# RWKV scan: order of TensorE's products among the inverses' steps, place of the bonus, buffers and time of y's factors

## The chip, the cores and the metric

One of the eight cores of a Trainium2 chip runs the whole program in one launch. The metric is the device time of that core in microseconds (us). Lines are those of the kernel before.

## The reference

The reference is a two-layer network on 256 tokens of width 1024, followed by a second block (window attention, stick-breaking attention, a PEER layer). The change touches only its RWKV-7 mixer in layer 0, with 16 heads of 64:

```
r, k, v = einsum(h + dx * mu[:3], w_rkv)
...
y = wkv7_scan(heads(r), heads(decay), heads(k), heads(v), -kk, kk * a_h)
mean = mean(y, -1);  var = mean((y - mean)**2, -1)
y = ((y - mean) * rsqrt(var + eps)) * ln_g + ln_b
bonus = sum(heads(r) * heads(k) * r_k, -1)
y = y + bonus * heads(v)
return (y * g) @ w_o
```

The scan goes over the tokens with a state of 64x64 per head. The kernel computes it in two blocks of 128 tokens (tb 0 and 1) by matrices: the token-by-token products MAK, MRK, MRB and MT (masked), the inverse of a unit lower triangular matrix made of MT (TIT is its transpose), then w, u = TIT w, the state S0 between the blocks, and y.

## The kernel before, in words

All weights stream as 128x1024 tiles (512 KB each, line 164, from SyncE's queue) through four raw slots. ScalarE makes the rounded high part of each (line 182), VectorE the low part (line 194; from `in_q_a` on every third on GpSimd, line 206), and TensorE multiplies with both (lines 252 to 254, 295 to 299). w_v's tiles are used whole. No tile scheduler is involved: each engine has its order written out by hand, and engines meet at semaphores.

TensorE's order in the scan stands in `tensor_scan`. The inverses come in steps of a generator, `tensor_inverses`: X5 of both blocks (line 952, 32x32 products), then TIT5 and TI5 (lines 964 and 966), X6 of block 0 in two halves (line 975), X6 of block 1 together with TIT6 of block 0 (lines 975 and 978), and TIT6 of block 1 (line 978). ScalarE takes block 0's results out (line 1560), VectorE block 1's (line 1290), and each step needs the one before taken out. "Products" MAK, MRK and MRB (line 933) are 16 small matmuls for each block and kind, taken out with a mask by VectorE in four pieces (line 1285). w, u and y are added by `add` (line 1053): eight matmuls of 128x128 weights on 64 columns for a half. Every matmul of plain f32 stands as two instructions in the trace, so w of a half has 16. `tensor_bonus` (line 870) has 16 matmuls, 32 instructions.

PSUM has eight banks, handed out in turn by `bank` (line 230): who takes a bank waits until its last content, eight banks ago, has been taken out. So any insertion or move in TensorE's order changes who waits for whom.

GpSimd makes the factors of y in `pool_factors`: four operations on 128x1024 for each block (lines 1640, 1643, 1645, 1647), once the gains `ln` have been loaded (line 754, 1 MB, issued after the bonus is done and after the first four tiles of w_o).

VectorE's order in the scan stands in `vector_scan`: after the inverses, the masks of MRK and MRB of block 0, the low parts of w_o's first three tiles (line 194, after ScalarE has made the high parts behind u of block 0), the state S0 (lines 1309 and 1314), centring (lines 1342 to 1349), the twelve masks of block 1, y's norm.

Of the kernel before, what the change touches and what calls it, by code (L numbers as in the profile page):

```python
# [16 lines left out]
P = 128  # L17
# [653 lines left out]
def rwkv_rooms(k):  # L671
# [13 lines left out]
        b_tok=u(1)[:, 0:D], k_tok=u(1)[:, D:2 * D], S0=u(1)[:, 0:D], wbuf=late[:, 0, 0:D], ubuf=late[:, 0, D:2 * D],  # L685
        ln=late[:, 1, :], y=u(5)[:, 0:D], y2=u(5)[:, D:2 * D], u=u,
        MT=matrices(arena[:, 9:11, :], P), TIT=matrices(arena[:, 12:14, :], P), TI=matrices(arena[:, 14:15, :], HD),
        MAK=[matrices(arena[:, n:n + 1, :], P) for n in (5, 11)], MRB=[matrices(arena[:, 9 + tb:10 + tb, :], P) for tb in range(TB)],
        MRK=[matrices(arena[:, 0:1, :], P)] * TB, X5=matrices(r["spare"][:, 0:1, 0:D], SMALL),
        X6=matrices(r["spare"][:, 1:2, :], HD), diagonal=u(5)[:, 0:D].rearrange("p (q t) -> p q t", t=SMALL), blocks=u(11)[:, 0:D].rearrange("p (i j) -> p i j", j=SMALL),  # L690
# [71 lines left out]
def tensor_rwkv(k):  # L762
# [175 lines left out]
def tensor_inverses(k):  # L938
# [7 lines left out]
    for tb in range(TB):  # L946
# [6 lines left out]
        ins.then_inc(*k.level_products.mark(("X5", tb, 0), ("X5", tb, 1)))  # L953
    yield
    tensor.wait_ge(*k.small_turned.at("TIT"))
    for tb in range(TB):
# [10 lines left out]
        ins.then_inc(*k.level_products.mark(("TIT5", tb, 0), ("TIT5", tb, 1), ("TI5", tb)))  # L967
    yield
    low, up = rows_of(0, 2), rows_of(2, 2)
# [10 lines left out]
    for half in range(2):  # L980
        ps = bank(k, ("X6", 0, half), out[0], ("X6", 0, half))
        for m in range(8):
            ins = first(ps, 8 * half + m, slice(m * HD, (m + 1) * HD))
        ins.then_inc(*k.level_products.mark(("X6", 0, half)))
        yield
    tensor.wait_ge(*out[1].at(("TI5", 1)))
# [53 lines left out]
def tensor_scan(k):  # L1040
# [52 lines left out]
    def state():  # L1093
# [8 lines left out]
        ins.then_inc(*k.state_done.mark("state"))  # L1102

    inverses = tensor_inverses(k)
    next(inverses)
    tensor_bonus(k)
    next(inverses)
    w(0, 0)
    next(inverses)
    w(0, 1)  # L1110
    next(inverses)
    next(inverses)
    tensor_scan_tokens(k)
    next(inverses)
    tensor_scan_products(k, 0, "MRK", "k_s", "r_s", k.masked)
    tensor_scan_products(k, 0, "MRB", "b_s", "r_s", k.masked)
    for half in range(2):
        u(0, half)
    state()
    tensor_scan_products(k, 1, "MAK", "k_s", "a_s", k.masked)  # L1120
    for half in range(2):
        y(0, half, y_known(0, half))
    tensor_scan_products(k, 1, "MRB", "b_s", "r_s", k.masked)
    tensor_scan_products(k, 1, "MRK", "k_s", "r_s", k.masked)
    for half in range(2):
# [4 lines left out]
    known.append(y_known(1, 1))  # L1130
    for half in range(2):
        y(1, half, known[half])
    for half in range(2):
        tensor_turn_y(k, 0, half)

# [143 lines left out]
def vector_scan(k, substitute):  # L1279
# [16 lines left out]
    vector.transpose(r["straight"], r["inverse"].rearrange("p i j -> p j i")).then_inc(*k.small_turned.mark("TI"))  # L1296
    vector.transpose(r["turned"], r["inverse"]).then_inc(*k.small_turned.mark("TIT"))
    steps = take_out_inverses(k, 1, copy)
    next(steps)
    vector.wait_ge(*k.bonus_done.at("bonus"))  # L1300
    vector.tensor_copy(r["bonus"], result(k, "bonus")[:, 0:TB * HEADS]).then_inc(*k.scaled.mark("bonus"))
    for _ in steps:
        pass
    masked("MRK", 0, r["upto"])
    masked("MRB", 0, r["upto"])
    split_low(k, FIRST["w_o"][0] + SLOTS)
    S0, ps = r["S0"], result(k, "state")
    vector.wait_ge(*k.state_done.at("state"))
# [9 lines left out]
    vector_centring(k)  # L1318
    vector.wait_ge(*k.small_copied.at("TIT"))
    vector.wait_ge(*k.small_turned.now())  # L1320
    masked("MAK", 1, r["strict"])
    masked("MRB", 1, r["upto"])

    vector.wait_ge(*k.per_head_done.at(("y", 0, 1)))
    masked("MRK", 1, r["upto"])
    for _ in zip(vector_head_norm(k, 0), vector_head_norm(k, 1)):
        pass
    for half in range(2):
        vector_head_var(k, 1, half)
    for half in range(2):  # L1330
        vector_y_low(k, 0, half)
    for _ in zip(vector_last_norm(k, 0), vector_last_norm(k, 1)):
# [29 lines left out]
def vector_head_norm(k, half):  # L1362
# [21 lines left out]
    vector.wait_ge(*done.now())  # L1384
    vector.tensor_tensor(yh, yh, r["y2"][:, cols], ALU.add).then_inc(*k.y_made.mark((0, half)))
    yield


def vector_last_norm(k, half):
# [12 lines left out]
    vector.wait_ge(*done.now())  # L1402
    vector.tensor_tensor(yh, yh, r["y2"][:, cols], ALU.add).then_inc(*k.y_made.mark((1, half)))
    yield
# [145 lines left out]
def scalar_scan(k):  # L1550
# [12 lines left out]
    next(steps)  # L1563
    next(steps)
    for half in range(2):
        per_head("w", 0, half, r["wbuf"])
        next(steps)
    next(steps)
    for name, dst in (("b", r["b_tok"]), ("k", r["k_tok"])):
        for i in range(2):  # L1570
            scalar.wait_ge(*k.tokens_turned.at(name + str(i)))
            scalar.activation(dst[:, half_of(i)], result(k, ("tok", name, i)), ACT.Copy).then_inc(
                *k.tokens_out.mark((name, i)))
    for half in range(2):
        per_head("u", 0, half, r["ubuf"])
# [7 lines left out]
    for half in range(2):  # L1583
        per_head("u", 1, half, r["ubuf"])
    for half in range(2):
        scalar_head_squares(k, 1, half)
    for tb in range(TB):
        for half in range(2):
            scalar_y_high(k, tb, half)


def pool_rwkv(k):
# [17 lines left out]
    for quarter in (2, 3, 0, 1):  # L1610
# [3 lines left out]
        pool.wait_ge(*k.small_copied.now())  # L1614
    pool_factors(k, 0)
    for half in range(2):
        pool_head_root(k, 0, half)
    pool_factors(k, 1)
    for half in range(2):
        pool_head_root(k, 1, half)  # L1620

# [7 lines left out]
def pool_factors(k, tb):  # L1629

    pool, r, done = k.pool, k.room["rwkv"], k.factors_made
    g_of, y2 = r["g_tok"][:, tb, :], r["y2"]
    pool.wait_ge(*k.loaded["ln"].at("ln"))
    pool.wait_ge(*k.scaled.at("bonus"))
    pool.wait_ge(*k.v_out.at(("w_v", tb, 1)))
    if tb:
        pool.wait_ge(*k.y_made.at((0, 1)))
    else:
        pool.wait_ge(*k.per_head_done.at(("w", 0, 1)))
    pool.tensor_tensor(by_head(y2), by_head(r["v_tok"][:, tb, :]), spread(r["bonus"][:, tb * HEADS:(tb + 1) * HEADS], HD),  # L1640
                       ALU.mult).then_inc(*done.mark())
# [1640 lines left out]
```

## Time and profile before

| | |
|---|---|
| median of 3 runs | 2251.96 us (2251.47 to 2253.64) |
| profiled execution, own time | 2245.33 us |
| its span in the trace | 2244.0 us |
| TensorE busy | 2129.6 us, 95% of the span |
| VectorE, ScalarE, GpSimd busy | 1558.4, 1108.9 and 348.3 us |
| mean granted clock of TensorE | 0.963 of 2.4 GHz |

Times of the trace count from the start of the span. The RWKV mixer's scan lies between 335.8 us, when w_v's last product has been issued, and 422.9 us, when w_o's first starts. The granted clock is 1.00 (2.4 GHz) or 0.50 (1.2 GHz) at any time. A busy TensorE says little by itself: matmuls overlap, so the distance between starts counts.

### The profile page before, as it was taken

The numbers are of one execution on the slowest core, as the hardware profiler recorded it, in microseconds if no ns is written. First come the engines' busy times: TensorE is split into PE (matmuls) and PEld (weight loads), VectorE is DVE, ScalarE is ACT, GpSimd is POOL, SyncE is SP. The second block draws the span as 40 slices with busy tenths as digits, with TensorE's granted clock in tenths as the row PEclk, the third lists the DMA queues.
The fourth block names the chain that finished last, engine by engine and source line by source line (L and its number), as shares of the span: only waits on it lengthen the run. The fifth ranks groups of instructions, "written<-read, shape, count | busy, mean of one in ns | idle before, by whom it ended". The sixth has DMA issues, their size and how long they took to land.

```text
span 2244.0 us, 33802 instructions
## 1 busy us (share of the span) xinstructions
PE 2129.6 (95%) x13292; PEld 1861.4 (83%) x13292; DVE 1558.4 (69%) x2589; ACT 1108.9 (49%) x1757; POOL 348.3 (16%) x165
## 2 busy tenths in 40 slices
PE   8997999999999999799999878999999999999999
PEld 6886788888878887578888656999999999888887
DVE  5667784676676666866675775688999995555554
ACT  5554632265555555555554774444444444444443
POOL 0000102200010001100004102223222222222222
PEclk9998997999999999689999889999999999999999
DMA  5665231156645565146655224444544445656664
GB/s 197 190 188 178 85 113 58 50 181 187 192 161 181 192 187 173 45 126 192 188 186 192 86 66 156 163 161 160 170 150 142 145 142 175 196 195 192 193 191 158
DMA packets 97630, 352.52 MB, mean 157 GB/s; under 512 B 10897, under 2 KB 12689, under 8 KB 97089
## 3 DMA queue, kind: packets, MB, share of 16 engines
q1 hardware_dynamic: 97472, 350.36, 48.9%
q8 instruction: 107, 1.75, 0.3%
q14 instruction: 51, 0.41, 0.1%
HBM read 349.26 MB, written 1.05 MB: 156 GB/s over the span
## 4 chain that ended last, share of the span: by engine, by line
PE 81%; DVE 13%; ACT 3%; issue 2%; POOL 1%; DMA 0%; SPq 0%; ACTq 0%; DVEq 0%
PE psum L252 17%; PE psum L253 16%; PE psum L254 16%; PE psum L296 14%; PE psum L295 6%; DVE tile_low L194 3%; PE psum L2586 2%; PE psum L1053 1%; PE psum L856 1%; ACT tile_high L182 1%; PE psum L299 1%; POOL small L1665 1%; DVE hT L488 1%; PE psum L338 1%; DVE peer_active L2781 1%
## 5 line engine op out<-in xcount | busy, mean ns | idle before, releaser
L194 DVE TENSOR_TENSOR tile_low<-raw_tiles,tile_high 128x1024 fp32r<-128x1024 f32 x535 | 662.5, 1241 | 368.4 <-ACT tile_high L182 361.8
L182 ACT ACTIVATE tile_high<-raw_tiles 128x1024 fp32r<-128x1024 f32 x642 | 677.7, 1056 | 447.2 <-PE psum L254 447.0
L296 PE MATMUL psum<-hT,tile_high 128*128 128x512 f32 x1408 | 494.7, 395 | 5.6 <-issue 5.0
L206 POOL TENSOR_TENSOR tile_low<-raw_tiles,tile_high 128x1024 fp32r<-128x1024 f32 x107 | 269.9, 2522 | 761.9 <-ACT tile_high L182 761.9
L252 PE MATMUL psum<-hT,tile_high 128*128 128x256 f32 x1280 | 372.9, 291 | 8.0 <-DVE tile_low L194 3.9
L253 PE MATMUL psum<-hT,tile_high 128*128 128x256 f32 x1280 | 365.5, 286 | 0.0
L254 PE MATMUL psum<-hT,tile_low 128*128 128x256 f32 x1280 | 365.2, 285 | 0.0
L252 PE MATMUL psum<-tile_high,hT 128*128 128x512 f32 (+1 forms) x848 | 336.7, 397 | 22.6 <-DVE mix_arena L2402 9.3
L295 PE MATMUL psum<-hT,tile_low 128*128 128x256 f32 x1232 | 344.2, 279 | 0.0
L253 PE MATMUL psum<-tile_low,hT 128*128 128x512 f32 (+1 forms) x848 | 333.0, 393 | 0.0
L254 PE MATMUL psum<-tile_high,hT 128*128 128x512 f32 (+1 forms) x848 | 333.0, 393 | 0.0
L296 PEld LDWEIGHTS psum<-hT,tile_high 128*128 128x128 f32 x1408 | 258.9, 188 | 55.2 <-issue 6.1
L252 PEld LDWEIGHTS psum<-hT,tile_high 128*128 128x128 f32 x1280 | 249.0, 195 | 9.6 <-issue 8.0
L253 PEld LDWEIGHTS psum<-hT,tile_high 128*128 128x128 f32 x1280 | 249.2, 195 | 0.0
L254 PEld LDWEIGHTS psum<-hT,tile_low 128*128 128x128 f32 x1280 | 248.8, 194 | 0.0
L295 PEld LDWEIGHTS psum<-hT,tile_low 128*128 128x128 f32 x1232 | 232.8, 189 | 8.9
L252 PEld LDWEIGHTS psum<-tile_high,hT 128*128 128x128 f32 x848 | 162.4, 192 | 62.6 <-issue 15.1
L254 PEld LDWEIGHTS psum<-tile_high,hT 128*128 128x128 f32 x848 | 162.0, 191 | 33.8
L253 PEld LDWEIGHTS psum<-tile_low,hT 128*128 128x128 f32 x848 | 162.5, 192 | 32.5
L252 PE MATMUL psum<-tile_high,ffn_hidden_high 128*128 128x512 f32 x352 | 139.3, 396 | 2.5 <-DVE ffn_hidden_low L657 2.5
L253 PE MATMUL psum<-tile_low,ffn_hidden_high 128*128 128x512 f32 x352 | 139.0, 395 | 0.0
L254 PE MATMUL psum<-tile_high,ffn_hidden_low 128*128 128x512 f32 x352 | 139.0, 395 | 0.0
(334 smaller groups left out, 2541.8 us busy)
## 6 DMA issues: line engine op xcount, KB each, us to landing
raw_tiles<-ffn_in_dram SPq DMA_DIRECT2D x176, 512.0 KB, 3.6
raw_tiles<-peer_u_dram SPq DMA_DIRECT2D x128, 512.0 KB, 3.3
raw_tiles<-peer_v_dram SPq DMA_DIRECT2D x128, 512.0 KB, 4.0
raw_tiles<-ffn_out_dram SPq DMA_DIRECT2D x88, 512.0 KB, 3.5
raw_tiles<-w_kv_dram SPq DMA_DIRECT2D x16, 512.0 KB, 3.4
raw_tiles<-in_gates_dram SPq DMA_DIRECT2D x16, 512.0 KB, 3.3
raw_tiles<-peer_q_dram SPq DMA_DIRECT2D x16, 512.0 KB, 3.4
raw_tiles<-w_k_dram SPq DMA_DIRECT2D x8, 512.0 KB, 4.1
```

The costliest lines, as they stand in the source:

```text
L182: scalar.activation(k.high[:, n % SLOTS, :], k.raw[:, n % RAW_SLOTS, :], ACT.Copy).then_inc(*k.tile_high_made.mark(n))
L194: vector.tensor_tensor(k.low[:, n % SLOTS, :], k.raw[:, n % RAW_SLOTS, :], k.high[:, n % SLOTS, :].bitcast(F32), ALU.subtract).then_inc(*k ...
L206: pool.tensor_tensor(k.low[:, n % SLOTS, :], k.raw[:, n % RAW_SLOTS, :], k.high[:, n % SLOTS, :].bitcast(F32), ALU.subtract).then_inc(*k.p ...
L252: k.tensor.matmul(out, still[0], moving[0], start=first, stop=False)
L253: k.tensor.matmul(out, still[0], moving[1], start=False, stop=False)
L254: return k.tensor.matmul(out, still[1], moving[0], start=False, stop=last)
L295: k.tensor.matmul(ps[:, 0:T], low[:, c, :], both[:, c, 0, :], start=False, stop=False, skip_group_check=True)
L296: ins = k.tensor.matmul(ps, high[:, c, :], both[:, c, :, :], start=(c == 0), stop=(c == KC - 1), skip_group_check=True)
L299: k.tensor.matmul(ps[:, 0:T], low[:, c, :], both[:, c, 0, :], start=False, stop=False, skip_group_check=True)
L338: ins = k.tensor.transpose(ps[:, c * P:(c + 1) * P], src[:, c * P:(c + 1) * P], k.ident)
L488: vector.scalar_tensor_tensor(out=k.hT[1][:, c, :], in0=result(k, ("x", s, c))[:, 0:T], scalar=gain_of(k, s, c), in1=k.hT[0][:, c, :].bitc ...
L2586: ins = tensor.matmul(ps[:, n, :], r["i_hot"](q)[:, :, n], r["j_gates"](q)[:, n // 2, w, :, n % 2], start=(w == 0), stop=(w == PARTS - 1))
```

## The change

- `tensor_bonus` moves from behind X5 to between w_v's two halves.
- `tensor_inverses` pauses after each block's X5 and after each block's TIT5, and no more between the two halves of X6 of block 0: seven steps. Between them stand w(0,0), w(0,1), MRK of block 0, the turned tokens, MAK of block 1, MRB of block 0.
- MRB of block 1 comes before the state, MRK of block 1 between the state and y of block 0.
- MRK has two buffers (units 0 and 14), y2 too (units 5 and 4).
- GpSimd makes both blocks' factors before the first root. Block 1's wait for MRB of block 1 (the last reader of unit 4), where before they waited for y of block 0 to be finished.
- VectorE's masks follow the new order: MRB of block 1 stands between w_o's low parts and the state, MRK of block 1 behind the centring.
- y of block 0 is turned before the last products of y of block 1; ScalarE's and VectorE's orders follow.

```diff
-        MRK=[matrices(arena[:, 0:1, :], P)] * TB,
+        MRK=[matrices(arena[:, n:n + 1, :], P) for n in (0, 14)],
...
     for g in range(2):
+        if g:
+            tensor_bonus(k)
         ps = [bank(k, ("w_v", tb, g), k.v_out, ("w_v", tb, g)) for tb in range(TB)]
...
     inverses = tensor_inverses(k)
-    next(inverses)
-    tensor_bonus(k)
     next(inverses)
     w(0, 0)
     next(inverses)
     w(0, 1)
     next(inverses)
+    tensor_scan_products(k, 0, "MRK", "k_s", "r_s", k.masked)
     next(inverses)
     tensor_scan_tokens(k)
     next(inverses)
-    tensor_scan_products(k, 0, "MRK", "k_s", "r_s", k.masked)
+    tensor_scan_products(k, 1, "MAK", "k_s", "a_s", k.masked)
+    next(inverses)
     tensor_scan_products(k, 0, "MRB", "b_s", "r_s", k.masked)
+    next(inverses)
     for half in range(2):
         u(0, half)
+    tensor_scan_products(k, 1, "MRB", "b_s", "r_s", k.masked)
     state()
-    tensor_scan_products(k, 1, "MAK", "k_s", "a_s", k.masked)
+    tensor_scan_products(k, 1, "MRK", "k_s", "r_s", k.masked)
     for half in range(2):
         y(0, half, y_known(0, half))
-    tensor_scan_products(k, 1, "MRB", "b_s", "r_s", k.masked)
-    tensor_scan_products(k, 1, "MRK", "k_s", "r_s", k.masked)
     for half in range(2):
         w(1, half)
...
     for half in range(2):
+        tensor_turn_y(k, 0, half)
+    for half in range(2):
         y(1, half, known[half])
-    for half in range(2):
-        tensor_turn_y(k, 0, half)
...
     masked("MRK", 0, r["upto"])
+    next(steps)
+    vector.wait_ge(*k.small_copied.at("TIT"))
+    vector.wait_ge(*k.small_turned.now())
+    masked("MAK", 1, r["strict"])
+    next(steps)
+    next(steps)
     masked("MRB", 0, r["upto"])
+    next(steps)
     split_low(k, FIRST["w_o"][0] + SLOTS)
+    masked("MRB", 1, r["upto"])
     S0, ps = r["S0"], result(k, "state")
...
     vector_centring(k)
-    masked("MAK", 1, r["strict"])
-    masked("MRB", 1, r["upto"])
-    vector.wait_ge(*k.per_head_done.at(("y", 0, 1)))
     masked("MRK", 1, r["upto"])
...
-    pool_factors(k, 0)
-    for half in range(2):
-        pool_head_root(k, 0, half)
-    pool_factors(k, 1)
-    for half in range(2):
-        pool_head_root(k, 1, half)
+    for tb in range(TB):
+        pool_factors(k, tb)
+    for tb in range(TB):
+        for half in range(2):
+            pool_head_root(k, tb, half)
...
-    if tb:
-        pool.wait_ge(*k.y_made.at((0, 1)))
-    else:
-        pool.wait_ge(*k.per_head_done.at(("w", 0, 1)))
+    pool.wait_ge(*(k.scan_products.at(("MRB", 1, 1)) if tb else k.per_head_done.at(("w", 0, 1))))
```

## Rows read from the trace of the kernel before

**Rows 1.** The page: busy time of the engines, and the chain that ended last.

```profile
PE 2129.6 (95%) x13292; PEld 1861.4 (83%) x13292; DVE 1558.4 (69%) x2589; ACT 1108.9 (49%) x1757; POOL 348.3 (16%) x165
PE 81%; DVE 13%; ACT 3%; issue 2%; POOL 1%; DMA 0%; SPq 0%; ACTq 0%; DVEq 0%
```

**Rows 2.** Busy time of the engines, granted clock (PEclk) and DMA by stretches.

```profile
340.00:346.00 6.00, 6.00 (x40) 5.96 (x42) 1.16 (x3) 0.00 (x0) 1.82 (x1) 0.53 0.00 0
352.50:364.00 11.50, 11.44 (x80) 11.02 (x81) 2.05 (x3) 1.79 (x3) 1.71 (x1) 0.50 0.01 2
364.00:367.50 3.50, 3.50 (x65) 3.38 (x62) 0.72 (x2) 1.21 (x3) 3.34 (x3) 0.50 0.02 5
396.40:418.00 21.60, 21.60 (x195) 21.59 (x194) 12.27 (x23) 4.02 (x7) 8.11 (x5) 1.00 0.00 1
423.00:429.00 6.00, 6.00 (x14) 4.75 (x15) 4.26 (x7) 0.00 (x0) 2.38 (x2) 0.50 0.00 0
```

**Rows 3.** Timeline of TensorE, inverses: start, us, what, count, idle before and releaser.

```profile
335.84 3.80 PE L952 MATMUL psum<-rwkv_spare,rwkv_arena 32*32 32x32 f32 x128
339.57 6.31 PE L870 MATMUL psum<-rwkv_masks,rwkv_late 128*128 128x16 f32 x32
...
352.56 0.26 PE L964 MATMUL psum<-rwkv_arena,rwkv_spare 32*32 32x32 f32 x1 [2.63 <-issue]
...
352.94 3.68 PE L1053 MATMUL psum<-rwkv_arena 128*128 128x64 f32 x16
356.54 1.97 PE L975 MATMUL psum<-rwkv_arena 64*64 64x64 f32 x16
...
369.38 2.08 PE L978 MATMUL psum<-rwkv_arena,rwkv_spare 64*64 64x64 f32 x32
```

**Rows 4.** DMA issues between 345 and 352 us: KB, us to landing.

```profile
rwkv_late<-ln_dram SPq DMA_DIRECT2D x1, 1024.0 KB, 5.0
```

**Rows 5.** Timeline of TensorE, from the products to w_o.

```profile
371.39 3.84 PE L933 MATMUL psum<-rwkv_arena 64*128 64x128 f32 x64
...
379.72 0.34 PE L1100 MATMUL psum<-rwkv_late,rwkv_arena 128*64 128x64 f32 x4 [0.78 <-ACT rwkv_late L1555]
...
381.76 2.06 PE L933 MATMUL psum<-rwkv_arena 64*128 64x128 f32 x32
...
393.23 3.25 PE L933 MATMUL psum<-rwkv_arena 64*128 64x128 f32 x48 [1.04 <-DVE rwkv_arena L1285]
396.41 10.93 PE L1053 MATMUL psum<-rwkv_arena 128*128 128x64 f32 x96
...
422.94 0.77 PE L252 MATMUL psum<-tile_high,hT 128*128 128x512 f32 x1 [3.99 <-DVE hT L1423]
```

**Rows 6.** Timeline of VectorE between 380 and 400 us.

```profile
380.69 3.50 DVE L194 TENSOR_TENSOR tile_low<-raw_tiles,tile_high 128x1024 fp32r<-128x1024 f32 x3 [3.22 <-ACT tile_high L182]
384.35 0.91 DVE L1309 MEMSET rwkv_arena<- 128x1024 f32 x1 [0.16 <-issue]
...
391.80 7.26 DVE L1285 TENSOR_TENSOR rwkv_arena<-psum,rwkv_masks 128x512 f32<-128x512 f32 x12
```

**Rows 7.** Timeline of GpSimd: two of the four operations of block 1's factors.

```profile
413.01 1.90 POOL L1640 TENSOR_TENSOR rwkv_arena<-rwkv_arena,small 128x1024 f32<-128x1024 f32 x1 [3.81 <-DVE rwkv_arena L1385]
414.99 2.35 POOL L1643 TENSOR_TENSOR rwkv_arena<-rwkv_arena,rwkv_late 128x1024 f32<-128x1024 f32 x1
```

**Rows 8.** GpSimd and VectorE side by side, at 1503 us and at 1541 us.

```profile
1503.39 2.38 POOL L206 TENSOR_TENSOR tile_low<-raw_tiles,tile_high 128x1024 fp32r<-128x1024 f32 x1 [4.53 <-ACT tile_high L182]
...
1503.81 3.05 DVE L194 TENSOR_TENSOR tile_low<-raw_tiles,tile_high 128x1024 fp32r<-128x1024 f32 x1
...
1541.43 1.22 DVE L194 TENSOR_TENSOR tile_low<-raw_tiles,tile_high 128x1024 fp32r<-128x1024 f32 x1
1542.56 3.42 DVE L2781 TENSOR_TENSOR peer_active<-peer_active 128x1024 f32<-128x1024 f32 x1
...
1541.63 3.28 POOL L206 TENSOR_TENSOR tile_low<-raw_tiles,tile_high 128x1024 fp32r<-128x1024 f32 x1 [4.73 <-ACT tile_high L182]
```

More of the change, by code:

```diff
@@ L685, in rwkv_rooms @@
         b_tok=u(1)[:, 0:D], k_tok=u(1)[:, D:2 * D], S0=u(1)[:, 0:D], wbuf=late[:, 0, 0:D], ubuf=late[:, 0, D:2 * D],
-        ln=late[:, 1, :], y=u(5)[:, 0:D], y2=u(5)[:, D:2 * D], u=u,
+        ln=late[:, 1, :], y=u(5)[:, 0:D],
+        y2=(u(5)[:, D:2 * D], u(4)[:, 0:D]), u=u,
         MT=matrices(arena[:, 9:11, :], P), TIT=matrices(arena[:, 12:14, :], P), TI=matrices(arena[:, 14:15, :], HD),
         MAK=[matrices(arena[:, n:n + 1, :], P) for n in (5, 11)], MRB=[matrices(arena[:, 9 + tb:10 + tb, :], P) for tb in range(TB)],
-        MRK=[matrices(arena[:, 0:1, :], P)] * TB, X5=matrices(r["spare"][:, 0:1, 0:D], SMALL),
+        MRK=[matrices(arena[:, n:n + 1, :], P) for n in (0, 14)], X5=matrices(r["spare"][:, 0:1, 0:D], SMALL),
         X6=matrices(r["spare"][:, 1:2, :], HD), diagonal=u(5)[:, 0:D].rearrange("p (q t) -> p q t", t=SMALL), blocks=u(11)[:, 0:D].rearrange("p (i j) -> p i j", j=SMALL),
@@ L953, in tensor_inverses @@
         ins.then_inc(*k.level_products.mark(("X5", tb, 0), ("X5", tb, 1)))
-    yield
+        yield
     tensor.wait_ge(*k.small_turned.at("TIT"))
@@ L967, in tensor_inverses @@
         ins.then_inc(*k.level_products.mark(("TIT5", tb, 0), ("TIT5", tb, 1), ("TI5", tb)))
-    yield
+        yield
     low, up = rows_of(0, 2), rows_of(2, 2)
@@ L984, in tensor_inverses @@
         ins.then_inc(*k.level_products.mark(("X6", 0, half)))
-        yield
+    yield
     tensor.wait_ge(*out[1].at(("TI5", 1)))
@@ L1297, in vector_scan @@
     vector.transpose(r["turned"], r["inverse"]).then_inc(*k.small_turned.mark("TIT"))
+    vector.wait_ge(*k.bonus_done.at("bonus"))
+    vector.tensor_copy(r["bonus"], result(k, "bonus")[:, 0:TB * HEADS]).then_inc(*k.scaled.mark("bonus"))
     steps = take_out_inverses(k, 1, copy)
     next(steps)
[L1300 to L1303, printed above, removed]
     masked("MRK", 0, r["upto"])
+    next(steps)
[4 more added lines that the diff above has]
+    next(steps)
     masked("MRB", 0, r["upto"])
+    next(steps)
     split_low(k, FIRST["w_o"][0] + SLOTS)
+    masked("MRB", 1, r["upto"])
     S0, ps = r["S0"], result(k, "state")
@@ L1318, in vector_scan @@
     vector_centring(k)
-    vector.wait_ge(*k.small_copied.at("TIT"))
-    vector.wait_ge(*k.small_turned.now())
-    masked("MAK", 1, r["strict"])
-    masked("MRB", 1, r["upto"])
-    vector.wait_ge(*k.per_head_done.at(("y", 0, 1)))
     masked("MRK", 1, r["upto"])
@@ L1328, in vector_scan @@
     for half in range(2):
+        vector_y_low(k, 0, half)
+    for half in range(2):
         vector_head_var(k, 1, half)
-    for half in range(2):
-        vector_y_low(k, 0, half)
     for _ in zip(vector_last_norm(k, 0), vector_last_norm(k, 1)):
@@ L1384, in vector_head_norm @@
     vector.wait_ge(*done.now())
-    vector.tensor_tensor(yh, yh, r["y2"][:, cols], ALU.add).then_inc(*k.y_made.mark((0, half)))
+    vector.tensor_tensor(yh, yh, r["y2"][0][:, cols], ALU.add).then_inc(*k.y_made.mark((0, half)))
     yield
@@ L1402, in vector_last_norm @@
     vector.wait_ge(*done.now())
-    vector.tensor_tensor(yh, yh, r["y2"][:, cols], ALU.add).then_inc(*k.y_made.mark((1, half)))
+    vector.tensor_tensor(yh, yh, r["y2"][1][:, cols], ALU.add).then_inc(*k.y_made.mark((1, half)))
     yield
@@ L1563, in scalar_scan @@
     next(steps)
-    next(steps)
     for half in range(2):
         per_head("w", 0, half, r["wbuf"])
-        next(steps)
     next(steps)
@@ L1573, in scalar_scan @@
                 *k.tokens_out.mark((name, i)))
+    for _ in steps:
+        pass
     for half in range(2):
@@ L1585, in scalar_scan @@
     for half in range(2):
+        scalar_y_high(k, 0, half)
+    for half in range(2):
         scalar_head_squares(k, 1, half)
-    for tb in range(TB):
-        for half in range(2):
-            scalar_y_high(k, tb, half)
+    for half in range(2):
+        scalar_y_high(k, 1, half)
 def pool_rwkv(k):
@@ L1614, in pool_rwkv @@
         pool.wait_ge(*k.small_copied.now())
-    pool_factors(k, 0)
-    for half in range(2):
-        pool_head_root(k, 0, half)
-    pool_factors(k, 1)
-    for half in range(2):
-        pool_head_root(k, 1, half)
+    for tb in range(TB):
+        pool_factors(k, tb)
+    for tb in range(TB):
+        for half in range(2):
+            pool_head_root(k, tb, half)
 def pool_head_root(k, tb, half):
@@ L1631, in pool_factors @@
     pool, r, done = k.pool, k.room["rwkv"], k.factors_made
-    g_of, y2 = r["g_tok"][:, tb, :], r["y2"]
+    g_of, y2 = r["g_tok"][:, tb, :], r["y2"][tb]
     pool.wait_ge(*k.loaded["ln"].at("ln"))
```

## The prediction

> **What bounds the kernel now.** The page comes first: TensorE is busy for 95% of the span and makes 81% of the chain that ended last [rows 1]. So time is won or lost where TensorE waits or runs at the low clock, and the scan is such a place. The stretches show how [rows 2]: from 340 us on, in the bonus, the granted clock is 0.50 and stays there past 364 us; it is 1.00 from 396 to 418 us; it is 0.50 again behind a wait. The timeline shows what TensorE did before each fall: 3.8 us of 32x32 products before the first [rows 3], a gap of 3.99 us before the second [rows 5]. Gaps of 0.78 and 1.04 us between such products caused none [rows 5]. How it rises matters as much. In 352.5 to 364 us, 32 of the scan's 128x64 products ran back to back and the clock did not move [rows 2, 3]; the same products kept it at 1.00 in 396 to 418 us. They hold a clock that is high and don't bring it back. Their price differs by two: 3.68 us for 16, or 0.230 each, at 0.50 [rows 3], 10.93 us for 96, or 0.114 each, at 1.00 [rows 5].
>
> **The front: inverses, up to u of block 0.** The bonus among w_v's dense products runs at 1.00; its 32 instructions load 128x128 weights, so I price them as 0.114: 3.65 us for 6.31 [rows 3, 5], -2.7. The idle 2.63 us at 352.56, where TensorE waits for nothing that is shown, lies in the 5.0 us in which the 1 MB of ln lands [rows 3, 4]; I read it as TensorE's own instructions arriving behind ln. Now ln goes out just after w_o's fourth tile, at about 340 us, and the many small products of TIT5 come near 347: -2.6 (bounds 0 and -2.6, as the load is only 7 us away).
>
> X5, w(0,0), X5, w(0,1), TIT5: half of this is still 32x32 work, of the kind ahead of the fall at 340 us. I take it that the clock falls once here, after w(0,0), and that MRK of block 0 and the turned tokens bring it back. So w(0,0) gains 3.68 - 1.82 = 1.9, w(0,1) nothing. X6 of block 0 goes from 2 x 1.97 to the 2.08 that TIT6 of block 1 takes at 1.00 [rows 3], -1.9; X6 of block 1 with TIT6 of block 0 from 3.5 to half [rows 2], -1.7. MRK of block 0 costs 1.9 at 1.00 (half of 3.84 [rows 5]) and twice that at 0.50: +1.9. The bonus, 3.65 us of light work, may drop the clock under w_v: nothing shows it; bounds 0 and 3.0, half of the 6 us of dense products at 0.50 behind 423 us [rows 2]; I take 1.0, a third, since one short stretch of light work may or may not be enough. MAK of block 1 moves in from behind, at no net cost. VectorE's masks and copies lie in these steps' shadows. Sum of the front: -2.7 - 2.6 - 1.9 - 1.9 - 1.7 + 1.9 + 1.0 = **-7.9** (-12.7 if the clock never falls; +5.5 if it stays low, with three kinds of products at +1.9 each, TIT6 of block 1 at +2.1, the bonus at 3.0, and only -2.7 and -2.6 gained).
>
> **The back: from T, the end of u of block 0.** Before, T is 379.72 - 0.78 = 378.94 us [rows 5]. MRB of block 1 now covers u's way out, -0.8, and the wait of 1.04 for a bank between the products goes, -1.0.
>
> What takes its place is on VectorE and GpSimd. The low parts of w_o's three tiles start at T + 1.75 and end at T + 5.25 [rows 6]; their start is set by ScalarE behind u. GpSimd's factors of block 1 wait for MRB of block 1, so they start at T + 1.9: into the middle of them. Two engines with operations of two SBUF inputs don't run at once. At 1503 us a low part that began 0.4 us after GpSimd's takes 3.05 us instead of 1.22 and ends 1.1 us after GpSimd's 2.38 us are over; at 1541 us GpSimd waits for one VectorE operation, and then the next VectorE operation waits for GpSimd's whole one [rows 8]. They take turns. So: first low part done at T + 2.97, GpSimd's first (1.90 [rows 7]) at 4.8, second low part at 5.9, GpSimd's second (2.35) at 8.2, third low part at 9.3. Then come the masks of MRB of block 1, 0.605 us apart [rows 6], the first read out at T + 10.0.
>
> TensorE needs that first mask at once. Count the banks in the new order: MRB of block 1 takes numbers 47 to 50, the state 51, MRK of block 1 52 to 55. Number 55 is bank 7 and so is 47, so MRK's second half waits until MRB's first piece is out. TensorE gets there at T + 1.9 (MRB) + 2.0 (state, from 379.72 to 381.76) + 0.96 (half of MRK) = T + 4.9, and goes on at T + 10.1: a gap of 5.2 us, **+5.2**. It is longer than the one of 3.99 us that took the clock down. Behind it stand, in instructions of line 1053, y of block 0 (64), w of block 1 (64), the known part of y of block 1 (64), u (32) and the last part of y (32): 256, none of which raises it, 256 x (0.230 - 0.114) = **+29.7**. MRK's second half +1.0, the eight transposes of y of block 0 +0.9 (a 128x128 weight each).
>
> The state's chain, from the memset to the centring's end, takes 391.80 - 384.35 = 7.45 us [rows 6]; behind four masks it ends at T + 19.3. TensorE at 0.50 reaches w of block 1 at T + 26.7: no wait. Turning y of block 0 ahead of the last products takes away the wait of 3.99 us before w_o, **-4.0**. Roots behind both factors cost nothing: factors end near T + 14, ScalarE's squares come after w of block 1. w_o's first products ran at 0.50 before [rows 2] and will again, 0. Second buffers for MRK and y2 free waits that the new order would otherwise have. Sum of the back: -1.8 + 5.2 + 29.7 + 1.0 + 0.9 - 4.0 = **+31.0**.
>
> Together -7.9 + 31.0 = +23.1 us on the profiled execution's 2245.3, 2268.4. That execution lies 6.6 us under the median of the runs; added to the median it is 2275.
>
> **A rule against this.** The rows say that back-to-back 128x64 products leave the clock at 0.50 [rows 2, 3]. The Trainium skill, "TensorE: Matmul & The Clock Gate", Part 1, says that a sustained busy stretch of matmuls releases the throttle, whatever is issued. By that rule y's own products would end the low stretch, which is the second rival below; the trace disagrees at 352 to 364 us.
>
> **Rivals.** (1) *GpSimd does not hold up the low parts*: they end at T + 5.25 as before, because VectorE keeps the port between operations. Then MRK's second half waits until T + 6.05, a gap of 1.15, and w of block 1 meets the centring at T + 15.35 instead of 14.3, another 1.05. Gaps of that size left the clock up [rows 5], and w_o's start gains half of its 6 us at 0.50: -7.9 - 1.8 + 1.15 + 1.05 - 4.0 - 3.0 = -14.5, **2237**, faster. It decides at one point: whether the three low parts are over by T + 5.5. Against it speaks 1541 us, where VectorE had the next operation ready and GpSimd went first. (2) *The clock comes back in y*, after 6 us as behind 423 us: -7.9 - 1.8 + 5.2 + 3.0 - 4.0 - 3.0 = -8.5, **2243**. (3) *As (1), but the gap of 1.05 us, with half-dense products on both sides, drops the clock*: 192 instructions at +0.116 are 22.3, the turns 0.9, and w_o's start gains nothing: -14.5 + 3.0 + 22.3 + 0.9 = +11.7, **2264**. The gap of 1.04 before had denser products around it, so this is open. (4) *The change does not do what it says*: full products between the small steps don't lift the clock, the front costs 5.5 instead of gaining, and with the back it is +36.5, 2288.
>
> **How the numbers follow.** The forecast has 0.70, rival 1 0.12, rival 2 0.09, rival 3 0.05, rival 4 0.04. The forecast's own range is 2266 (front -12.7, and the transposes bring the clock back before y's last 32 products, -3.7) to 2285 (the front gives back most of what it gains). For 8 in 10 the range has to take in rivals 3 and 2 as well: 2240 to 2285. What a measurement of this kernel can tell from no change is 0.2%, 4.5 us. Faster: rivals 1 and 2, 0.21, of which 0.01 may end within that bound; slower: the forecast and rivals 3 and 4, 0.79, of which 0.02 may. That leaves 0.20, 0.03 and 0.77.
>
> **What would show it.** GpSimd's L1640 group of block 1 starts within 0.3 us of MRB's end, and a low part (L194) beside it lasts about 3 us. An idle of about 5 us stands before L933's last 16 products, released by L1285. The clock is 0.50 from there until w_o, and L1053 at 0.23 each for 16 halves. No 2.6 us of "issue" in TIT5. No wait at w_o's first product. It is wrong if the low parts stay at 1.22 us, if the gap is near 1 us, or if the clock reads 1.00 in y of block 0.

## The result, and the profile after

Six executions of the changed kernel have a median of 2265.73 us (2263.52 to 2274.56), six of the kernel before beside them 2251.72 us: a ratio of 1.0068, 95% interval 1.0051 to 1.0084. The change makes the kernel slower by 14 us, on the side that was forecast and 9 us less than the forecast's 2275. The profiled execution took 2263.52 us; all readings below are of it and stand against the profiled execution of before, 2245.33 us. Three executions far outside the rest, one each of run 2 (3482 us), run 4 (2388 us) and the kernel before (8512 us), are left out of the ratios.

The page of the changed kernel, busy time of the engines [rows 1]:

```profile
PE 2152.1 (95%) x13292; PEld 1883.1 (83%) x13292; DVE 1559.6 (69%) x2589; ACT 1109.2 (49%) x1757; POOL 351.1 (16%) x165
```

TensorE runs as many instructions and is busy 22.5 us longer. The busy share, 95% in both, does not show the loss; the stretches of the changed kernel do (the column behind the engines' busy times is the granted clock) [rows 2]:

```profile
324.50:327.90 3.40, 3.40 (x8) 2.01 (x7) 3.06 (x11) 0.00 (x0) 0.00 (x0) 0.50 0.00 0
345.00:355.00 10.00, 10.00 (x167) 9.53 (x163) 2.72 (x5) 2.36 (x4) 5.68 (x3) 0.50 0.02 7
355.20:372.60 17.40, 17.40 (x331) 16.68 (x323) 10.55 (x17) 5.03 (x9) 3.11 (x2) 1.00 0.01 2
376.70:382.40 5.70, 1.11 (x17) 0.92 (x16) 5.70 (x4) 0.00 (x0) 5.54 (x3) 1.00 0.49 179
398.20:432.00 33.80, 33.80 (x161) 33.80 (x160) 7.23 (x13) 4.02 (x7) 3.27 (x2) 0.50 0.00 0
```

In the front the low clock, which lasted from 340 to 367.5 us [rows 2], shrank to 345 to 355 us: it ends as MRK of block 0 does. A new low stretch stands under w_v, behind the bonus, from 324.5 to 327.9 us. Behind u of block 0 TensorE is busy 1.1 of 5.7 us, and then the clock is 0.50 for the whole rest of the scan. The timeline of TensorE of the changed kernel [rows 3, 5]:

```profile
320.38 3.64 PE L873 MATMUL psum<-rwkv_masks,rwkv_late 128*128 128x16 f32 x32
...
341.46 2.00 PE L1056 MATMUL psum<-rwkv_arena 128*128 128x64 f32 x16
...
372.60 2.06 PE L936 MATMUL psum<-rwkv_arena 64*128 64x128 f32 x32
...
382.51 2.08 PE L936 MATMUL psum<-rwkv_arena 64*128 64x128 f32 x16 [4.70 <-DVE rwkv_arena L1289]
384.52 3.67 PE L1056 MATMUL psum<-rwkv_arena 128*128 128x64 f32 x16
...
398.23 20.69 PE L1056 MATMUL psum<-rwkv_arena 128*128 128x64 f32 x96
...
432.36 1.92 PE L338 MATMUL psum<-ident,rwkv_arena 128*128 128x128 f32 x8
434.07 6.93 PE L1056 MATMUL psum<-rwkv_late,rwkv_arena 128*128 128x64 f32 x32
...
448.45 0.50 PE L252 MATMUL psum<-tile_high,hT 128*128 128x512 f32 x1 [0.98 <-DVE hT L1427]
```

And the kernel before, at the end of the scan, where w_o goes on behind the second turn of y:

```profile
417.90 1.04 PE L338 MATMUL psum<-ident,rwkv_arena 128*128 128x128 f32 x8
...
432.02 0.50 PE L252 MATMUL psum<-tile_high,hT 128*128 128x512 f32 x1 [0.97 <-DVE hT L1423]
```

T, the end of u of block 0, is 372.60 us for 378.94, 6.3 us earlier. Not all of that is the change: the products just ahead of w_v, up to which the two kernels' orders on TensorE are the same, already start 1.56 us earlier. The changed kernel, and the kernel before:

```profile
304.49 2.06 PE L936 MATMUL psum<-rwkv_arena 64*128 64x128 f32 x32
```

```profile
306.05 2.06 PE L933 MATMUL psum<-rwkv_arena 64*128 64x128 f32 x32
```

From there to T it takes 372.60 - 304.49 = 68.1 us for 378.94 - 306.05 = 72.9: the front gained 4.8 us. This distance is steadier than T itself: in run 7, whose front is that of the kernel before, T comes 3.7 us later, and the distance is 72.9 us again. From T to the point where w_o goes on it takes 448.45 - 372.60 = 75.9 us for 432.02 - 378.94 = 53.1: the back lost 22.8 us. With the early start (-1.6) and 1.8 us more behind that point, which nothing here explains, these make up the 18.2 us between the two executions.

VectorE and GpSimd of the changed kernel behind T, two timelines [rows 6, 7]:

```profile
374.42 7.35 DVE L194 TENSOR_TENSOR tile_low<-raw_tiles,tile_high 128x1024 fp32r<-128x1024 f32 x3 [4.64 <-ACT tile_high L182]
381.69 2.47 DVE L1289 TENSOR_TENSOR rwkv_arena<-psum,rwkv_masks 128x512 f32<-128x512 f32 x4
```

```profile
374.84 2.57 POOL L1642 TENSOR_TENSOR rwkv_arena<-rwkv_arena,small 128x1024 f32<-128x1024 f32 x1 [16.45 <-PE psum L936]
377.49 3.20 POOL L1645 TENSOR_TENSOR rwkv_arena<-rwkv_arena,rwkv_late 128x1024 f32<-128x1024 f32 x1
```

The three low parts take 7.35 us instead of 3.50, GpSimd's own operations 2.57 and 3.20 instead of 1.90 and 2.35, as they would if the two take turns. The first mask of MRB comes at T + 9.1 us, and MRK's second half waits 4.70 us for its bank.

### The profile page after: what moved, and what is told of

The parts are those of the page before. It is cut to its first block, busy times and chain, and to the rows that moved or that the text cites. A ratio compares the mean times of both kernels' runs of the same rounds, so it can differ in the third digit from the quotient of the medians.

```text
span 2262.2 us, 33801 instructions
## 1 busy us (share of the span) xinstructions
PE 2152.1 (95%) x13292; PEld 1883.1 (83%) x13292; DVE 1559.6 (69%) x2589; ACT 1109.2 (49%) x1757; POOL 351.1 (16%) x165
## 4 chain that ended last, share of the span: by engine, by line
PE 82%; DVE 12%; ACT 3%; issue 1%; POOL 1%; DMA 0%; SPq 0%; ACTq 0%; DVEq 0%
PE psum L252 17%; PE psum L254 16%; PE psum L253 16%; PE psum L296 14%; PE psum L295 6%; DVE tile_low L194 3%; PE psum L1056 3%; PE psum L2588 2%; PE psum L859 1%; ACT tile_high L182 1%; PE psum L299 1%; POOL small L1667 1%; DVE hT L488 1%; PE psum L338 1%; DVE peer_active L2783 1%
```

## The experiments

The kernel before ran beside each group; ratios are to it, with their 95% interval. Times that an expectation names stand on the scale of the profiled executions (2245.33 us before, 2263.52 changed); a measured time is the median, to be held against medians of 2250 to 2252 us for the kernel before and 2265.73 for the changed one. Where an expectation gives a ratio, that is the fairer comparison. "T" is the start of MRB of block 1 or the end of u of block 0 in each profile.

**1. The low parts later** (low_late)

```diff
     next(steps)
-    split_low(k, FIRST["w_o"][0] + SLOTS)
     masked("MRB", 1, r["upto"])
...
     masked("MRK", 1, r["upto"])
+    split_low(k, FIRST["w_o"][0] + SLOTS)
```

> Edit: only the low parts of w_o's first three tiles move, on VectorE, from ahead of the masks of MRB of block 1 to behind those of MRK of block 1. Theory (the gap of 4.70 us ahead of MRK's second half drops the clock, and the low clock is the loss): VectorE takes MRB out at once, no gap of over 0.5 us behind u of block 0, the clock stays at 1.00 up to w_o. Saved against the changed kernel's profiled 2263.5: gap 4.7, 256 instructions of L1056 at 0.213 - 0.114 = 25.3, MRK's second half 1.0, turns 0.9, w_o's start 3: 2229, a ratio to the kernel before near 0.993. Rival A (the clock falls in any case, since state, MRK and y are light work): only the gap goes, 2259. Rival B (low parts come too late for w_o, or raw slots come free too late): a new wait before w_o's first products and part of the gain given back.

Measured: median 2252.58 us, ratio 0.998 (0.995 to 1.0015). The twelve executions lie in two heaps: five at 2229.9 to 2238.2 us and seven at 2252.4 to 2261.4. The profiled one is of the upper heap. Its TensorE, and its VectorE and GpSimd:

```profile
384.20 1.95 PE L1056 MATMUL psum<-rwkv_late,rwkv_arena 128*128 128x64 f32 x16
386.79 18.87 PE L1056 MATMUL psum<-rwkv_arena 128*128 128x64 f32 x96 [0.64 <-DVE rwkv_arena L1353]
```

```profile
382.00 2.25 DVE L1350 TENSOR_SCALAR small<-small 128x32 f32<-128x32 f32 x1
```

```profile
381.87 2.35 POOL L1649 TENSOR_TENSOR rwkv_arena<-rwkv_arena,rwkv_late 128x1024 f32<-128x1024 f32 x1
```

The gap of 4.70 us is gone, but a new one of 0.64 us stands before w of block 1, and the clock falls behind it: 96 instructions take 18.87 us instead of 10.9. Its cause is a VectorE operation on 128x32 numbers that takes 2.25 us: it begins 0.13 us after GpSimd's last factor operation and ends with it. The reductions and the masks from PSUM beside GpSimd's other three took their usual 1.2 and 0.6 us. The Trainium skill, "SBUF — State Buffer", section "Who interferes with whom", has this: a VectorE `tensor_scalar` from SBUF can need the port pair that GpSimd uses, a reduction never does, and who comes second waits for the whole instruction of the other. The rows agree. The lower heap is where I expected the time (2229). Its five executions have a mean granted clock of 0.967 to 0.969, the seven of the upper heap 0.952 to 0.959, so it is the clock that parts them. Only an execution of the upper heap was profiled: that the lower ones have the same gap and keep the clock behind it is inferred.

**2. GpSimd's factors later** (pool_late)

```diff
-    pool.wait_ge(*(k.scan_products.at(("MRB", 1, 1)) if tb else k.per_head_done.at(("w", 0, 1))))
+    pool.wait_ge(*(k.state_made.at("centred") if tb else k.per_head_done.at(("w", 0, 1))))
```

> Edit: only GpSimd's factors of block 1 wait for the centring instead of for MRB of block 1, so nothing of GpSimd lies beside the three low parts. Theory (GpSimd's two-input operations held up the low parts): the low parts last 1.22 us each again (L194 x3 takes 3.5 us instead of 7.35), the gap ahead of MRK's second half shrinks from 4.70 to about 1.1, w of block 1 waits about 1.0 for the centring. If gaps of that size leave the clock up, 2231 profiled; if the 1.0 us gap between 128x64 products on both sides drops it there, 192 instructions at +0.099 and what follows: about 2254. Rival (the low parts are slow for another reason): 2263 as the changed kernel.

Measured: 2252.27 us, ratio 1.0006 (0.9993 to 1.0019). The profiled execution took 2247.53 us, where 2254 was expected if the second gap drops the clock. VectorE and TensorE:

```profile
375.25 3.50 DVE L194 TENSOR_TENSOR tile_low<-raw_tiles,tile_high 128x1024 fp32r<-128x1024 f32 x3 [4.64 <-ACT tile_high L182]
```

```profile
379.50 1.16 PE L936 MATMUL psum<-rwkv_arena 64*128 64x128 f32 x16 [0.85 <-DVE rwkv_arena L1289]
...
388.86 19.29 PE L1056 MATMUL psum<-rwkv_arena 128*128 128x64 f32 x96 [0.92 <-DVE rwkv_arena L1353]
...
423.31 4.28 PE L1056 MATMUL psum<-rwkv_late,rwkv_arena 128*128 128x64 f32 x32
```

```profile
425.00:427.00 2.00, 2.00 (x21) 2.00 (x19) 0.53 (x1) 0.60 (x1) 0.00 (x0) 1.00 0.00 0
```

The low parts are back at 3.50 us with nothing else changed: GpSimd held them up, which was the theory. The first gap is 0.85 us and leaves the clock up; the second, 0.92 us with 128x64 products on both sides, is followed by 0.50. That is the mechanism of the forecast's third rival, though its 2264 was 12 us too high. One thing here speaks against a rule that I had taken as firm. Behind the eight transposes of y of block 0 the clock came back among the last 128x64 products of y of block 1: 32 of them took 4.28 us, and it is 1.00 from 425 us on. In the changed kernel and in runs 1 and 3 the same 32 stayed at 0.50 (6.93 us). So 128x64 products mostly leave a low clock low, but not always; what made the difference here is not shown.

**3. The gap filled with work** (gap_filled). Nothing is left out: the first half of MRK of block 1 is computed five times into the same banks.

```diff
-        for i in range(4):
+        for i in [i for _ in range(5 if (kind, tb, gg) == ("MRK", 1, 0) else 1) for i in range(4)]:
```

> Edit: in the changed kernel the first half of MRK's products of block 1 is computed five times instead of once, into the same banks, so TensorE works through most of the 4.70 us in which it waited; nothing else moves and the second half starts at the same time (4 x 1.0 to 1.2 us of added work fill 4.0 to 4.7 us). Theory (idle time, not the kind of work, drops the clock): clock 1.00 up to w_o, 25.3 + 1.0 + 0.9 + 3 = 30 us less: 2233 to 2235 with not a microsecond of waiting removed. Rival (the clock would fall behind MRK anyway, or the time lies in the wait itself): 2263 or a little more.

Measured: 2259.3 us, ratio 1.003 (1.0015 to 1.0047): 6.4 us under the changed kernel's median, not 30. Its profiled execution (2268.85 us) reached T 8 us late, so only distances are read:

```profile
384.51 4.74 PE L936 MATMUL psum<-rwkv_arena 64*128 64x128 f32 x80
390.39 1.16 PE L936 MATMUL psum<-rwkv_arena 64*128 64x128 f32 x16 [1.14 <-DVE rwkv_arena L1289]
391.48 2.00 PE L1056 MATMUL psum<-rwkv_arena 128*128 128x64 f32 x16
...
399.76 20.05 PE L1056 MATMUL psum<-rwkv_arena 128*128 128x64 f32 x96 [0.92 <-DVE rwkv_arena L1353]
```

I had missed what the quick y of block 0 uncovers. With the gap filled but for 1.14 us, the clock stays at 1.00 through y (16 instructions in 2.00 us, not 3.67), TensorE arrives at w of block 1 earlier than the centring, waits 0.92 us, and the clock falls there. So 64 instructions, MRK's second half (0.9 us), and no more are saved: 64 x 0.099 + 0.9 = 7.2 us, less the 0.9 of the new wait, 6.3. From T to the point where w_o goes on the trace has 449.36 - 380.46 = 68.9 us for the changed kernel's 75.9, 7.0 less. That the medians differ by 6.4 is no check of this sum: the ten executions lie between 2251.6 and 2268.9 us.

**4. Dense products behind the gap** (dense_behind). Nothing is left out; the second half of MRK is computed five times (the edit of 3 with `("MRK", 1, 1)`).

> Edit: in the changed kernel the second half of MRK's products of block 1 (64x128, behind the gap) is computed five times instead of once: 64 more instructions. Theory (full 64x128 products bring the clock back, 128x64 products don't): the clock rises within these 5 x 2.08 us or less, y of block 0 and all behind it run at 1.00; added 4 to 8 us, saved 25.3 + 0.9 + 3: 2239 to 2243. Rival (the low stretch ends by something else, such as w_o's 512-column products): 8.3 us more, 2272.

Measured: 2241.71 us, ratio 0.995 (0.9937 to 0.9968). TensorE's timeline, and a stretch:

```profile
382.60 6.36 PE L936 MATMUL psum<-rwkv_arena 64*128 64x128 f32 x80 [4.71 <-DVE rwkv_arena L1289]
...
396.09 10.88 PE L1056 MATMUL psum<-rwkv_arena 128*128 128x64 f32 x96
```

```profile
383.00:386.40 3.40, 3.40 (x36) 3.40 (x35) 3.17 (x6) 0.00 (x0) 3.32 (x2) 0.50 0.38 143
386.40:389.00 2.60, 2.60 (x47) 2.48 (x44) 2.50 (x3) 0.00 (x0) 0.10 (x1) 1.00 0.03 6
```

The gap is the same, 4.71 us. The clock falls, and it rises again while the 64x128 products run; from there to w_o it is 1.00. Sixty-four added instructions make the kernel 24 us faster than the changed one by the medians; from T to the point where w_o goes on the trace has 424.98 - 372.69 = 52.3 us for 75.9. With the gap as long as before, that isolates the price of the low clock behind it, and shows that 80 of the 64x128 products brought it back where the changed kernel's 16 of them, and 56 us of 128x64 products with eight transposes among them (384.5 to 440.8 us), did not.

**5. Both late** (no_gap): the edits of 1 and 2 together.

> Edit: the changed kernel with both earlier edits together: GpSimd's factors of block 1 behind the centring, and VectorE's low parts of w_o's three tiles behind the masks of MRK of block 1. Each alone left one or two gaps of 0.64 to 0.92 us in front of 128x64 products, and the clock fell there in the profiled runs. Theory (any idle time of that size among 128x64 products can drop the clock, and without one they hold it): L1350 takes 0.18 us instead of 2.25, the centring ends about 1.5 us before w of block 1 wants it, no gap from u of block 0 to w_o, clock 1.00 to w_o in every run: 2229 to 2232 in all executions, ratio near 0.991, and none of the two-peaked times of the low parts' edit alone. Rival (the long light stretch drops the clock by itself): 2250 or again two peaks.

Measured: 2241.9 us (2238.7 to 2246.3), ratio 0.9966 (0.9953 to 0.9979). One heap, but 10 us over what I expected. VectorE and TensorE:

```profile
386.74 9.73 DVE L194 TENSOR_TENSOR tile_low<-raw_tiles,tile_high 128x1024 fp32r<-128x1024 f32 x3
```

```profile
385.72 10.88 PE L1056 MATMUL psum<-rwkv_arena 128*128 128x64 f32 x96
...
406.87 1.94 PE L338 MATMUL psum<-ident,rwkv_arena 128*128 128x128 f32 x8 [3.12 <-DVE rwkv_arena L1389]
```

Without a gap, 25 us of 128x64 products, up to 403.7 us, leave the clock at 1.00: the length of such a stretch alone does not take it down. That holds for these products only. In the front of the changed kernel the clock fell without any wait of TensorE, behind 32x32 products (at 345 us) and behind the bonus (at 324.5 us). But I had moved the collision instead of removing it. The low parts now meet all four factor operations (9.73 us), the norm of y of block 0 is late, TensorE waits 3.12 us before its turn, and the clock falls there: the 32 last 128x64 products take 6.93 us again.

**6. The front alone** (front_only): behind u of block 0 everything as before.

```diff
-    tensor_scan_products(k, 1, "MRB", "b_s", "r_s", k.masked)
     state()
-    tensor_scan_products(k, 1, "MRK", "k_s", "r_s", k.masked)
     for half in range(2):
         y(0, half, y_known(0, half))
+    tensor_scan_products(k, 1, "MRB", "b_s", "r_s", k.masked)
+    tensor_scan_products(k, 1, "MRK", "k_s", "r_s", k.masked)
```

> Edit: the changed kernel with everything behind u of block 0 as before (MRB and MRK of block 1 behind y of block 0, masks, roots, factors of block 1 and the turn of y in the old order), so only the front's changes are left (bonus, interleaving, MAK of block 1 early, buffers). Theory (the front was worth 6.3 us in the profiled execution, and the loss lies behind u alone): T is 6 us earlier, MAK masks being out early takes away the wait of 1.04 us, clock 1.00 through y and w, the wait of about 4 us before w_o stays: 2238, ratio 0.997. Rival (the early gain is only a matter of when the scan starts, 1.5 us of it at least): 2240 to 2244. Rival (the front's order leaves the clock nearer to its fall): a fall in y and 2255 or more.

Measured: 2237.93 us, ratio 0.9954 (0.9937 to 0.9971), where 0.997 was expected; the profiled execution took 2237.74 us, where 2238 was expected.

```profile
373.82 0.34 PE L1103 MATMUL psum<-rwkv_late,rwkv_arena 128*64 128x64 f32 x4 [0.78 <-ACT rwkv_late L1559]
...
413.45 0.58 PE L252 MATMUL psum<-tile_high,hT 128*128 128x512 f32 x1 [4.01 <-DVE hT L1427]
```

The front's half of the change is a gain by itself, of 0.3 to 0.6%; the waits of 0.78 and 4.01 us are those of before, and the one of 1.04 us is gone. Which of the front's parts bring the gain is not separated here; run 8 tries one of them.

**7. The early turn alone** (turn_early): the kernel before, with y of block 0 turned before the last products.

> Edit: the kernel before, with only y of block 0 turned ahead of the last products of y of block 1 (and ScalarE's and VectorE's order for it). Theory: the wait of 3.99 us before w_o's first product goes, and with it the fall of the clock over w_o's first 6 us: 4.0 + 3.0 = 7.0 us less, 2238. Rival (y of block 0's low part is late all the same, because VectorE comes to it later than TensorE): the wait only moves ahead of the turn or shrinks to 2 us, clock falls again, 2243.

Measured: 2250.23 us, ratio 0.9993 (0.9979 to 1.0006), no difference that can be told.

```profile
429.24 0.72 PE L338 MATMUL psum<-ident,rwkv_arena 128*128 128x128 f32 x4 [2.42 <-DVE rwkv_arena L1403]
430.84 1.08 PE L338 MATMUL psum<-ident,rwkv_arena 128*128 128x128 f32 x4 [0.88 <-DVE rwkv_arena L1403]
```

The wait of 3.99 us went, and 3.30 us came up one step later, at the turn of y of block 1, whose norm on VectorE now ends last; the low clock moved there too (0.50 from 431 to 435 us). From T to the end of w_o's products, the start of line 459, the trace has 69.0 us for 70.9 before, so 2 us were gained, not 7, and the medians can't tell that. Part of the norm's delay is once more the collision of VectorE and GpSimd. Two operations of VectorE on 128x8 numbers, 0.17 us each in run 9, are held up by GpSimd's late factors of block 1 and end with them, at 423.6 and 426.1 us:

```profile
422.24 1.34 DVE L1417 TENSOR_SCALAR small<-small 128x8 f32<-128x8 f32 x1
...
424.21 1.86 DVE L1417 TENSOR_SCALAR small<-small 128x8 f32<-128x8 f32 x1
```

**8. The bonus alone** (bonus_moved): the kernel before, with `tensor_bonus` between w_v's halves.

> Edit: the kernel before, with only the bonus moved between w_v's two halves. Theory: the bonus costs 3.65 instead of 6.31 us (2.7 less), and ln goes out behind w_o's fourth tile, so TensorE's 2.63 us without a shown wait in TIT5 vanish or go elsewhere: 2245.3 - 2.7 - 2.6 = 2240, ratio 0.998. Rival A (the stall has nothing to do with ln): 2242.6. Rival B (32x32 products now meet each other without the bonus between, X5's way out is no longer covered): the gain is eaten by a wait of 1 to 2 us before TIT5.

Measured: 2249.66 us, ratio 0.9997 (0.9985 to 1.001). TensorE, and a stretch:

```profile
322.21 3.64 PE L872 MATMUL psum<-rwkv_masks,rwkv_late 128*128 128x16 f32 x32
...
345.38 0.27 PE L966 MATMUL psum<-rwkv_arena,rwkv_spare 32*32 32x32 f32 x2 [1.90 <-issue]
...
347.73 0.26 PE L966 MATMUL psum<-rwkv_arena,rwkv_spare 32*32 32x32 f32 x2 [0.99 <-issue]
...
351.13 0.26 PE L966 MATMUL psum<-rwkv_arena,rwkv_spare 32*32 32x32 f32 x1 [0.56 <-issue]
```

```profile
342.00:344.00 2.00, 1.48 (x54) 1.32 (x48) 0.47 (x1) 0.89 (x2) 0.19 (x1) 1.00 1.04 385
346.60:347.80 1.20, 0.21 (x9) 0.07 (x6) 0.00 (x0) 0.00 (x0) 0.00 (x0) 0.50 0.02 7
```

The bonus costs 3.64 us as priced, but 3.45 us without a shown wait stand in TIT5, in three pieces. The first lies beside full DMA engines (share 1.04, ln); the second has next to none beside it (0.02). So ln is at most part of the cause. From the products ahead of w_v to T it takes 70.5 us for 72.9: 2.4 less, not 5.3, and too little for the medians to tell.

**9. The last factor late** (last_factor_late): edit 1, and of block 1's four factor operations only the last behind the centring.

```diff
     pool.wait_ge(*done.now())
+    if tb:
+        pool.wait_ge(*k.state_made.at("centred"))
     pool.tensor_tensor(g_of, g_of, r["ln"][:, 0:D], ALU.mult).then_inc(*done.mark(tb))
```

> Edit: the changed kernel with VectorE's low parts of w_o's three tiles behind the masks of MRK of block 1, and of GpSimd's four factor operations of block 1 only the last behind the centring; the first three stay behind MRB of block 1, where VectorE has only masks, copies from PSUM and reductions, which ran beside them unhindered. Theory: GpSimd's third operation ends at 381.8 us, just before VectorE's L1350 at 381.9, so L1350 takes 0.18 us, the centring is early, no gap behind u; the low parts last 3.5 us, not 9.73 (as with both edits before), y of block 0 is normed before its turn (no 3.12 us wait), the clock is 1.00 to w_o, and only y of block 1's norm keeps TensorE waiting, some 6.7 us behind its last product of which w_o's first tiles cover 4: second turn and on at 415 us instead of 421.3 with the front alone. 2237.7 - 6.3 = 2231, ratio 0.992. Rival (one more thing in the way: the low parts meet the fourth operation, or the norm is still late): a wait of 1 to 3 us before y of block 0's turn and a low clock into w_o: 2238 to 2242.

Measured: 2235.04 us (2228.57 to 2236.33), ratio 0.9922 (0.9908 to 0.9936): the fastest version, 17 us under the kernel before (expected: ratio 0.992). VectorE and TensorE:

```profile
382.95 0.18 DVE L1350 TENSOR_SCALAR small<-small 128x32 f32<-128x32 f32 x1
...
387.95 3.48 DVE L194 TENSOR_TENSOR tile_low<-raw_tiles,tile_high 128x1024 fp32r<-128x1024 f32 x3
```

```profile
386.94 10.88 PE L1056 MATMUL psum<-rwkv_arena 128*128 128x64 f32 x96
...
413.79 0.63 PE L338 MATMUL psum<-ident,rwkv_arena 128*128 128x128 f32 x4 [0.24 <-DVE rwkv_arena L1407]
```

Both collisions are gone, there is no gap behind u, and the clock is 1.00 into w_o.

**10. Front and turn** (front_and_turn): the kernel of 6 with the early turn.

> Edit: the front's changes and the early turn of y of block 0, the rest behind u as before (the kernel with the front alone, plus the turn). Theory (from the turn alone on the kernel before: the wait before w_o only moved to y of block 1's second turn, where VectorE's norm and GpSimd's late factors end last, and the low clock went with it): from u's end to that turn 48.9 - 2.0 (MAK) - 1.0 (bank) = 45.8 us, against 48.3 with the front alone, of which the low clock takes 2.5 back: 2236 to 2238, the same as the front alone within 2 us. Rival (my first step: the wait of 4 us is gone for good, and the clock stays up): 2231.

Measured: 2238.03 us, ratio 0.9934 (0.992 to 0.9948); the kernel of 6 had 2237.93. The wait is again at the second turn (2.41 and 0.98 us). So the early turn brings nothing that can be told where the norm of y of block 1 ends last; in 9, where the factors were made long before, the same waits are 0.24 and 0.70 us.

## Why the prediction was right, and where its sizes were off

The mechanism was right step by step in the back, where the loss arose: the low parts collide with the factors (7.35 us; run 2 takes the collision away alone), VectorE reaches MRB's masks late, MRK's second half waits for bank 7, the clock falls, and the 128x64 products of this kernel did not bring it back. Run 4 shows that the clock is the price: the same gap costs 24 us less when more 64x128 products follow it. The rule under it was weaker than I wrote. The 32 products of 352.5 to 364 us were not back to back: they are two groups of 16 with 64x64 products between them [rows 3]. And in run 2 the clock did come back among 128x64 products.

- **Front, forecast -7.9.** From the products ahead of w_v, T came 4.8 us earlier with 2.0 us of MAK added ahead of it, so -6.8. (T by itself moved by 6.3, which with MAK would be 8.3, but 1.6 of that lies ahead of the change.) The bonus is 3.64 us for the forecast 3.65; w(0,0) runs at 1.00 and w(0,1) at 0.50, as taken; MRK of block 0 brings the clock back at 355 us. The bonus did drop the clock under w_v, for 3.4 us, so half of it, 1.7 us, where I took 1.0. It does so in five of the ten profiled executions that have the bonus there: from the bonus to X5 it takes 19.2 us in them and 17.5 in the other five.
- **The issue gap, -2.6.** It is gone in the changed kernel, but ln's move alone is not the reason, as I had it. Moving the bonus, and ln with it, leaves 3.45 us (run 8). The changed kernel has w(0,0) and w(0,1) between the small products; that this is what hides it was not tried.
- **The gap, +5.2.** 4.70 measured.
- **L1053 at the low clock, +29.7.** This is the term that was mis-sized most. The first 224 instructions take 432.36 - 384.52 = 47.84 us, and the last 32 take 440.75 - 434.07 = 6.68: 54.5 us for all 256, 0.213 each, where I took 0.230 from one group of 16 [rows 3], whose 3.68 us hold the start and the tail of the group too. Before, the same 256 took (391.03 - 383.74) + (417.90 - 396.41) = 28.8 us. So +25.7, 4.0 us less.
- **MRK's second half +1.0, turns +0.9.** 0.9 and 0.8.
- **w_o, -4.0.** From the end of y's products to the point where w_o goes on there were 14.1 us, 13.2 without the first turn; now there are 448.45 - 440.75 = 7.7: -5.5. The wait of 3.99 us is all gone, and the clock rises at 443.9 us, 3.1 us into w_o's products, where I had left their 6 us at 0.50 as before: 7.07 us for the first 18 became 5.69. No wait came up behind them, because GpSimd's factors of block 1 were early: with early factors at the full clock the second turn waits 0.94 us (runs 4 and 9), with late ones 3.3 (run 7).
- **Sum of the back, +31.0.** 22.8 + 2.0 for MAK = 24.8, 6.2 less than forecast: 4.0 of it is the mis-sized term, 1.5 w_o, 0.5 the gap, 0.2 MRK and the turns.
- **From one execution to the median.** I added 6.6 us because the profiled execution of before lay under its median. That of the changed kernel lies 2.2 us under its own, which is 4.4 us of the 9; the other 4.9 are the sum's. That no larger miss came of it owes something to luck: 1.1 us too much hoped for in the front stand against 6.2 too much feared in the back, and six executions of the changed kernel lie between 2263.5 and 2274.6 us.

Rival 1 said that without the collision the time is 2237 and that gaps of 1 us are harmless. The collision does not stay away by itself, and run 2 shows the second part wrong: without it the kernel takes 2252, rival 3's mechanism. Rival 2, the rule of the Trainium skill, "TensorE: Matmul & The Clock Gate", Part 1, that sustained matmuls release the throttle: the stretch from 384.5 to 440.8 us speaks against it for 128x64 products, run 4 for it with 64x128 ones. Run 2, where the clock came back among 128x64 products, keeps this from being a clean split by shape, and no run puts one shape in the place of the other. Rival 4 is refuted by run 6.

## What to carry to other kernels

A gap in front of light matmuls can cost the clock of all the light work behind it, and 0.6 to 0.9 us were enough here, though not every time; look for the last dense products before and the next ones behind it. When work is moved to another engine's idle time, write both engines' orders side by side and see which operations need two inputs from SBUF, or are a `tensor_scalar` from SBUF (runs 1 and 7): moving one of them away from a collision may only carry it to the next (run 5). A wait that a reordering removes is a gain only if the next thing waited for is earlier than it (run 7). Distances inside a trace compare better than points in it: T moved by 3.7 us between two executions whose kernels are the same up to there.

## What I had not expected

- The same program (run 1) takes 2230 to 2238 or 2252 to 2261 us, apparently by whether one gap of 0.64 us takes the clock down. Gaps of 0.78 us in run 6, 0.85 us in run 2, 1.04 us in the kernel before and 1.14 us in run 3 did not; 0.92 us in runs 2 and 3 did. Of these, the gaps that did stood with 128x64 products on both sides, those that did not in front of the state or of 64x128 products. Whether that or the moment of the gap decides stays open.
- A 128x32 `tensor_scalar` on VectorE can last 2.25 us instead of 0.18 beside a GpSimd operation (runs 1 and 9), on the path that TensorE waits for.
- Repeating products without need (run 4) makes the kernel 24 us faster than leaving them out.
- The clock can fall in one execution and not in another, with the programs the same up to there, also where TensorE never waits: behind the bonus it does so in five of ten profiles.
